# Half chunks at the start, two norms let past VectorE's splits, and a softmax mask moved from TensorE to VectorE

## The reference, cut to what matters

```python
for i in range(2):
    sh0, sc0, g0, sh1, sc1, g1, sh2, sc2, g2 = split(silu(c) @ mod_w[i] + mod_b[i], 9)
    x = x + 0.5 * g0 * swiglu(modulate(rms_norm(x, norm_g[i, 0]), sh0, sc0), ...)
    x = x + g1 * mixer(modulate(rms_norm(x, norm_g[i, 1]), sh1, sc1))   # pool, then attention
    x = x + 0.5 * g2 * swiglu(modulate(rms_norm(x, norm_g[i, 2]), sh2, sc2), ...)
x = rms_norm(x, final_g)
...
# the last layer's mixer: a causal attention of 8 heads of 64, beside an mLSTM branch
s_own = einsum('bhqd,bhkd->bhqk', qi, k_own) * scale
p = softmax(where(causal, s_own, -inf))
```

## Time and profile before

| what | value |
|---|---|
| median of 3 runs | 1464.5 us (1461.75 to 1464.64) |
| the profiled execution's own time | 1464.01 us |
| its span, first to last instruction | 1462.4 us |
| TensorE products busy | 1378.3 us, 94% of the span |
| VectorE busy | 931.0 us, 64% |
| ScalarE busy | 630.4 us, 43% |
| GpSimd busy | 179.5 us, 12% |
| TensorE waited for GpSimd's 1/rms matrix (L641 behind L2675) | 20.6 us in 6 waits |
| TensorE waited for the first chunk of `mod_w` (L612) | 10.0 us |
| TensorE waited for a chunk's sum on VectorE (L603 behind L1865) | 9.6 us in 2 waits |
| TensorE waited for the low part of an activation (L493 behind L2099) | 6.2 us in 3 waits |

### The profile page before, as it was taken

How to read it: one execution, slowest core, us unless ns; L and a number is a source line. 1 busy time by engine, 2 the same in 40 slices (tenths; PEclk the granted TensorE clock), 3 DMA queues, 4 the chain that set the end, 5 groups by cost and what they waited for, 6 DMA issues and landing times.

```text
span 1462.4 us, 18060 instructions
## 1 busy us (share of the span) xinstructions
PE 1378.3 (94%) x6431; PEld 1119.9 (77%) x6431; DVE 931.0 (64%) x1084; ACT 630.4 (43%) x821; POOL 179.5 (12%) x233
## 2 busy tenths in 40 slices
PE   6979999799999999999999799999799999999997
PEld 3668887688887788887777578888687777888885
DVE  4677777767777667777666465564677546555542
ACT  2433334443333544333565453433554645544341
POOL 2010002210001200011133010001208000000000
PEclk9989999899999999999999899999999999999999
DMA  9898886197886588884543275555436434455540
GB/s 337 283 333 293 297 304 226 58 326 278 298 297 216 180 309 288 288 303 139 165 140 95 85 281 173 184 193 189 145 116 209 144 124 136 157 175 177 198 170 29
DMA packets 179910, 304.82 MB, mean 208 GB/s; under 512 B 8516, under 2 KB 122580, under 8 KB 179592
## 3 DMA queue, kind: packets, MB, share of 16 engines
q1 hardware_dynamic: 159272, 224.62, 45.3%
q0 software_dynamic: 20576, 79.37, 15.0%
HBM read 302.91 MB, written 1.05 MB: 208 GB/s over the span
## 4 chain that ended last, share of the span: by engine, by line
PE 44%; DVE 3%; ACT 2%; POOL 1%; issue 1%; DMA 1%; SPq 0%; POOLq 0%; DVEq 0%; ACTq 0%
PE ps L493 13%; PE ps L495 12%; PE ps L494 12%; PE ps L641 1%; DVE wlo L1824 1%; PE ps L904 1%; PE ps L924 1%; PE ps L585 0%; ACT whi L1258 0%; PE ps L1147 0%; DMA raw<-in_ffn_w_gu 0%; DVE xres L2064 0%; DVE xn L2061 0%; DMA raw<-in_w_gate_up 0%; PE ps L1035 0%
## 5 line engine op out<-in xcount | busy, mean ns | idle before, releaser
L1824 DVE TENSOR_TENSOR wlo<-raw,whi 128x2048 fp32r<-128x2048 f32 x212 | 483.0, 2309 | 82.6 <-ACT whi L1258 82.4
L493 PE MATMUL ps<-whi,nthi 128*128 128x512 f32 (+1 forms) x1264 | 509.2, 403 | 7.8 <-DVE ntlo L2099 6.2
L494 PE MATMUL ps<-wlo,nthi 128*128 128x512 f32 (+1 forms) x1264 | 497.1, 393 | 0.0
L495 PE MATMUL ps<-whi,ntlo 128*128 128x512 f32 (+1 forms) x1264 | 496.4, 393 | 0.0
L1258 ACT ACTIVATE whi<-raw 128x2048 fp32r<-128x2048 f32 x212 | 397.0, 1909 | 83.8 <-DMA raw<-in_ffn_w_gu 41.9
L493 PEld LDWEIGHTS ps<-whi,nthi 128*128 128x128 f32 x1264 | 241.4, 191 | 58.4 <-issue 7.3
L495 PEld LDWEIGHTS ps<-whi,ntlo 128*128 128x128 f32 x1264 | 241.1, 191 | 51.7
L494 PEld LDWEIGHTS ps<-wlo,nthi 128*128 128x128 f32 x1264 | 241.7, 191 | 46.6 <-issue 0.2
L1865 DVE SCALAR_TENSOR_TENSOR arena<-arena,cact 128x512 f32<-128x512 f32 x238 | 181.9, 764 | 9.4
L493 PE MATMUL ps<-whi,hthi 128*128 128x512 f32 x440 | 174.8, 397 | 3.4 <-DVE htlo L1906 3.4
L495 PE MATMUL ps<-whi,htlo 128*128 128x512 f32 x440 | 172.1, 391 | 0.0
(11 more groups left out here) (252 smaller groups left out, 919.5 us busy)
## 6 DMA issues: line engine op xcount, KB each, us to landing
raw<-in_ffn_w_gu SPq DMA_DIRECT2D x176, 512.0 KB, 4.8
arena<-in_mod_w POOLq DMA_DIRECT2D x72, 1024.0 KB, 7.8
raw<-in_ffn_w_down SPq DMA_DIRECT2D x88, 512.0 KB, 5.8
raw<-in_w_in SPq DMA_DIRECT2D x44, 512.0 KB, 4.4
raw<-in_w_gate_up SPq DMA_DIRECT2D x44, 512.0 KB, 4.7
raw<-in_diff_w_qkv SPq DMA_DIRECT2D x24, 512.0 KB, 4.7
raw<-in_w_down SPq DMA_DIRECT2D x22, 512.0 KB, 5.6
raw<-in_diff_w_o SPq DMA_DIRECT2D x8, 512.0 KB, 4.1
```

The source lines that it names most:

```text
L493: pe.matmul(o, hi, wh, start=start, stop=False)
L494: pe.matmul(o, hi, wl, start=False, stop=False)
L495: return pe.matmul(o, lo, wh, start=False, stop=stop)
L1824: v.tensor_tensor(wlo[:, s * PIECE:(s + 1) * PIECE], raw[:, r * PIECE:(r + 1) * PIECE], hi, ALU.subtract).then_inc(w_lo, 1)
```

## The change

Four edits, and the moves of splits that go with them.

1. **Halves of chunks.** GpSimd's queue loads the first halves of chunks 2 and 0, then the second halves (before: chunk 0, then chunk 2); `load_gu` of piece 0 waits for the third of these four transfers, as before. Chunk 4 is added up in two halves in the middle of `first_head`, chunk 5 in two halves with a split between them at the end of `first_head`, and chunk 6 in two halves around `inner()` of the first step. Piece 3's split moves ahead of `keep_own_chunk`, the others move accordingly; there are 11 splits as before.
2. **The pool join.** The split at the end of `pool()` on VectorE goes to the end of `pool_join`, and between `joined(1)` and the first split VectorE waits for 1/rms of the first half.
3. **The join before the last mixer.** After `joined(1)` VectorE does `normalized(1)` at once and waits for the second 1/rms of that half; of the two splits ahead of it one comes after it and one later, after `keep(1, 0)`.
4. **The mask.** `scores(h)` loses the two mask products. `masked(h)` adds the mask in PSUM to both diagonal blocks in one operation of 128x256 values and waits for it before the maxima.

```diff
@@ scalar, first_head
                 n.next(M)
+                split(1)
                 act.wait_ge(xt_done, 4)
                 scaled_tiles(4, 2)
                 half_hi(0, 1)
                 half_hi(1, 1)
-                split(2)
+                split(1)
                 gated_half(0, full(T))
+                split(1)
                 gated_half(1, full(M))
...
@@ vector, first_head
                 add_chunk(3)
-                split(1)
+                split(2)
                 keep_own_chunk(chunk_at(*MOD_FIRST[1]))
                 keep_chunk(chunk_at(*MOD_FIRST[3]))
...
-                split(2)
+                split(1)
                 pass_by(T)
                 product(0, T)
+                c = add_chunk(halves=(0,))
                 pass_by(M)
                 product(1, M)
                 hidden_lo(0, 0, T)
+                split(1)
                 n.next(A)
                 product(0, A)
-                split(1)
                 hidden_lo(1, 0, M)
+                add_chunk(halves=(1,), of=c)
                 n.next(B)
                 product(1, B)
                 hidden_lo(0, 1, A)
                 split(1)
                 hidden_lo(1, 1, T)
                 split(1)
-                add_chunk()
-                split(1)
                 keep_chunk(chunk_at(*MOD_HEAD[0]))
+                c = add_chunk(halves=(0,))
+                split(1)
+                add_chunk(halves=(1,), of=c)
                 split(2)

             def ffn_steps(f):
-                if MOD_STEP[f]:
-                    add_chunk()
                 if len(MOD_STEP[f]) == 2:
                     keep_chunk(chunk_at(*MOD_STEP[f][0]))
-                    add_chunk()
-                inner()
+                    c = add_chunk(halves=(0,))
+                    inner()
+                    add_chunk(halves=(1,), of=c)
+                else:
+                    if MOD_STEP[f]:
+                        add_chunk()
+                    inner()
                 inner_lo(0)
...
@@ vector, pool_join
                 joined(0, last, (M, M))
-                n.next("rstd")
                 joined(1, last, (M, M))
+                dve.wait_ge(rstd_done, n.next("rstd").at + 1)
                 n.next("rstd")
                 split(1)
                 first_half(0, j, scol[:, :], shift)
                 x_lo(0)
-                split(2)
+                split(3)
...
@@ vector, join
                 joined(1, last, gated)
+                if final:
+                    normalized(1)
+                    dve.wait_ge(rstd_done, n.seen("rstd") + 1)
                 split(splits[2])
-                if final:
-                    normalized(1)
...
@@ vector, second_mix and masked
                 keep(1, 0, full(B))
-                split(2)
+                split(3)
...
                     o = full(A)
+                    diag = o.rearrange("p (a b k) -> p a b k", a=2, b=2)[:, :, 0, :]
+                    own.link(v.tensor_tensor(diag, diag, mask_q.unsqueeze(1).to_broadcast([P, 2, P]), ALU.add))
+                    own.wait()
                     own.link(v.tensor_reduce(top[:, c:c + 1], o[:, 0:P], AX.X, ALU.max, negate=True))
...
@@ tensor, scores
-                    pe.matmul(o[:, 0:P], qTa[rows, 0:P], kTa[rows, 0:P], start=True, stop=False)
-                    pe.matmul(o[:, 0:P], ident[:, :], mask_q, start=False, stop=True)
-                    pe.matmul(o[:, P:3 * P], qTa[rows, P:S], kTa[rows, 0:S], start=True, stop=False)
-                    pe.matmul(o[:, 2 * P:3 * P], ident[:, :], mask_q, start=False, stop=True).then_inc(filled[A], 1)
+                    pe.matmul(o[:, 0:P], qTa[rows, 0:P], kTa[rows, 0:P], start=True, stop=True)
+                    pe.matmul(o[:, P:3 * P], qTa[rows, P:S], kTa[rows, 0:S], start=True, stop=True).then_inc(filled[A], 1)
...
@@ gpsimd, the first transfers
-            for j in (0, 2):
-                load_own_chunk(*MOD_FIRST[j], j)
+            for h in range(2):
+                for j in (2, 0):
+                    load_own_chunk(*MOD_FIRST[j], j, halves=(h,))
```

More of the change, by code:

```diff
@@ L415, in ffn @@
                 if f == 0:
-                    load_gu(gu, 0, 0, [(first_landed[2][0], 16)])
+                    load_gu(gu, 0, 0, [(first_landed[2][1], 16)])
                     load_gu(gu, 1, 0)
@@ L1382, in ffn_head @@
                 one_hi(1, 0)
-                split(1)
+                split(2 if f == 1 else 1)
                 gated_half(0, full_at(A, p + 1))
@@ L1434, in first_head, with blocks_head @@
                 hidden_hi(0, 1, A)
-                split(2)
+                split(1)
                 hidden_hi(1, 1, T)
-                split(3)
-            def blocks_head(j, g_cols, p, keep):
+                split(4)
+            def blocks_head(j, g_cols, p, keep, ahead=1):
                 keep(0, 0, full(A))
@@ L1444, in blocks_head @@
                 pass_by(B)
-                split(1)
+                split(ahead)
                 keep(0, 1, full_at(A, p + 1))
@@ L1662, in others @@
                     nc.scalar.activation(dst, ps[:, 2 + (b + 1) % 2, :], func).then_inc(blk_read[1], 1)
-                blocks_head(j, (g_cols, None), START["in"], keep)
+                blocks_head(j, (g_cols, None), START["in"], keep, 2)
                 n.next(M)
@@ L1790, in _ @@
             norm = scol, mod_cols(0, 6)
-            j = join(*norm, (1, 0, 0, 2))
+            j = join(*norm, (0, 0, 0, 2))
             at = ffn(1, j, norm, True)
@@ L1802, in _ @@
             norm = cols[:, C_MIX:C_MIX + KT], None
-            j = join(*norm, (2, 1, 1, 1), squared=2, tail=at)
+            j = join(*norm, (2, 1, 1, 0), squared=2, tail=at)
             second_mix(j, norm[0])
@@ L1981, in first_head @@
                 split(1)
[L1982 removed]
+                keep_chunk(chunk_at(*MOD_HEAD[0]))
+                c = add_chunk(halves=(0,))
                 split(1)
[L1984 removed]
+                add_chunk(halves=(1,), of=c)
                 split(2)
             def ffn_steps(f):
[L1988 to L1989 removed]
                 if len(MOD_STEP[f]) == 2:
                     keep_chunk(chunk_at(*MOD_STEP[f][0]))
[L1992 to L1993 removed]
+                    c = add_chunk(halves=(0,))
[5 more added lines that the diff above has]
+                    inner()
                 inner_lo(0)
@@ L2141, in join @@
                 joined(1, last, gated)
-                split(splits[2])
                 if final:
                     normalized(1)
+                    dve.wait_ge(rstd_done, n.seen("rstd") + 1)
+                split(splits[2])
                 n.next("rstd")
@@ L2597, in _ @@
             ffn(3, j, norm, True)
-            j, norm = join(cols[:, C_MIX:C_MIX + KT], None, splits=(1, 1, 2), last=START["in"] - 1, final=True, tail=True)
+            j, norm = join(cols[:, C_MIX:C_MIX + KT], None, splits=(1, 1, 1), last=START["in"] - 1, final=True, tail=True)
             second_mix(j, norm)
@@ L2626, in load_chunk, with load_own_chunk @@
                         .then_inc(mod_landed[mod_place(c.first)][h], 16)
-            def load_own_chunk(layer, chunk, i, behind=()):
+            def load_own_chunk(layer, chunk, i, behind=(), halves=(0, 1)):
                 src = d["mod_w"][layer].rearrange("(k p) n -> p k n", p=P)
-                for h in range(2):
+                for h in halves:
                     if behind:
```

1 line of the change is left out of this document (removed).

## The result

| | before | changed |
|---|---|---|
| median | 1464.57 us (1461.75 to 1465.31, 4 runs) | 1454.33 us (1452.05 to 1454.67, 4 runs) |
| span of the profiled execution | 1462.4 us | 1452.6 us |
| products of 512 columns that took 0.60 to 0.66 us (half clock) | 72 | 56 |

The ratio is 0.9930, with an interval of 0.9916 to 0.9944. The kernel is 10.2 us faster. The forecast was 1448.8 us, a gain of 15.2, in a range of 1442 to 1458. The direction and the range held; the gain was forecast half as large again as it is.

The account below looks back on a forecast made before the run. TensorE, busy for 94% of the span, was taken as the bound, so only removing its work or waits pays. Terms: -5.0 - 3.4 - 0.9 - 5.9 = -15.2 us; 1464.0 - 15.2 = 1448.8 us, range 1442 to 1458.

Parts of the forecast that it names:

- The start, forecast -5.0: Halves of chunks at the start: later first product, no wait for chunk 4, earlier chunk 6; -5.0 us, bounds 0 and -9.
- the sum of chunk 6: At the start, TensorE's sum of chunk 6 comes at 97.3 instead of 103.72, with VectorE as the bound: -6.4 us.
- The pool join, forecast -3.4: Pool join: GpSimd's matrix is done at 278.8 instead of 282.3; -3.4 us, bounds -1.2 and -5.0.
- the matrix goes in between the last join operation and the split: Pool join: GpSimd's matrix runs after VectorE's last join operation and before its split, done at 278.2 + 0.6 = 278.8.
- meets the split: Pool join, lower bound: GpSimd's matrix collides with VectorE's split, and the edit gives only -1.2 us.
- piece 38: Behind the pool join: its load goes out later but lands before ScalarE's gated half, so no cost was put for it.
- The last join, forecast -0.9: Join before the last mixer: normalized(1) starts 3.0 us earlier, the matrix loses 2.1 to a split; -0.9 us, bounds -0.9 and -3.0.
- the tie: Last join: VectorE's split and GpSimd's matrix start on the same signal; the split was taken to win, +2.1 us.
- Rival (a): Last join: the matrix wins the tie by issue order, another -2.1 us, 1446.7 us; chance 20%.
- The mask, forecast -5.9: Last mixer: TensorE saves 0.75 us a head in eight heads by losing the mask products; -5.9 us, bounds -4.4 and -6.0.
- The cover: Last mixer: VectorE's 2.03 us wait before each head's split hides the added mask operation; only 0.1 given back at head 1.
- Rival (b): The start gives nothing, since waits for chunks 5 and 6 move to transfers: 1453.8 us; chance 18%.

Follow-up runs that it names:

- mask_only: The kernel before with only the mask edit, the mask added in PSUM by VectorE: 1455.07 us, ratio 0.9950.
- start_only: The kernel before with only the halves of chunks at the start, joins and mask as before: 1461.22 us, ratio 0.9976.
- no_pool_join: The changed kernel with the pool join as before (split ahead of the join operations, no wait for 1/rms): 1456.26 us, ratio 0.9937 to the kernel before.
- matrix_first: The changed kernel, but VectorE waits in both joins until GpSimd's matrix is done, not only 1/rms: 1450.36 us, ratio 0.9907 to the kernel before.
- quarter_lo: The changed kernel with the low part beside the matrix made in four operations instead of one in both joins: 1452.30 us, ratio 0.9916 to the kernel before.

## Why the prediction was right, and where it wasn't

**The start, forecast -5.0.** The steps came as written: first product 2.4 us later (2.9 said), the kept chunk waited for, no wait for chunk 4, the sum of chunk 6 within 0.9 us of its forecast, half clock behind it (from -7.3 at chunk 6 to -4.6 at the loop, a loss of 2.7 where 1.4 was put). But the term is mis-sized. It was priced against one execution of the kernel before, in which a piece landed 3.2 us later than in mask_only and which stands 2.5 us behind that one at 121 us. Over all profiles the edit is worth about 2.0 us at 121 us, and by the times of start_only 3.5 (1.9 to 5.1). Of the changed kernel's own 4.6, 1.7 went again at the end of the first part: the same wait of 1.39 us at 221 left the clock at full (1.00) where in the kernel before it was half (0.54 from 227 to 230), but TensorE only met its next wait sooner, 1.68 us for VectorE's product at 232.67, and the half level came there. Four kernels with the same two waits kept the clock, so this loss can stay away; what decides it is open.

**The pool join, forecast -3.4.** This is the step that failed, "the matrix goes in between the last join operation and the split". The mean fell into the join operation that reads PSUM, as said, and the power began in its last 0.1 us, and that was too early: 1/rms was done before the last operation, so VectorE never stood still, and there was no gap for the matrix. It "meets the split", which was the bound of -1.2; the squares at 288 moved by 1.2. A second step failed unseen: what waits behind the join was priced at nothing. The text looked at piece 38 alone, and no wait of TensorE came of that one. But ScalarE's moved high part (piece 39) held its low part back by 1.38 us and with it the load of piece 42 (310.64), and that load held the gated half: 2.0 to 3.75 us were given back. From 261 to 338 us the changed kernel's two profiles lose 2.5 and 0.8 us. Four profiles with the join as before (no_pool_join, start_only, mask_only and the kernel before) moved by -0.4 to 0.9 in this stretch. By the profiles the edit gave nothing or cost a little; by the times the changed kernel and its repetition are 1.0 to 1.6 us ahead of no_pool_join, inside the noise. Its worth as a whole stays open, and 3.4 us is in neither.

**The last join, forecast -0.9.** Right in its mechanism: the tie was lost, 2.70 us, wait 1.0 shorter. 0.5 was kept; part of the rest went into transposes of 3.79 instead of 3.43 us. Rival (a), the matrix wins, didn't occur, but forced by a wait in matrix_first its 2.1 us were all there, and 0.5 more (0.4 of it in shorter transposes, 3.41 us). By the Trainium skill (SBUF — State Buffer, Who interferes with whom) the shared ports belong for a whole instruction to whoever issues first. Here VectorE was first, by 0.07 us, and the trace agrees; the near tie of the earlier trace rows remains the other way round.

**The mask, forecast -5.9.** 6.7 us, in all kernels with it but quarter_lo (5.5; why is open). The cover was there: the addition took 0.43 us, close to the earlier trace rows, and of TensorE's longer waits only the one behind head 1's exponentials grew, from 0.30 to 0.48 us, about the 0.1 that was put for it. The size is 0.84 us a head instead of 0.75, since I took only the two starts of the mask products: the score product between them fell from 0.62 to 0.53 us as well.

**What wasn't in the sum.** This part is luck. 2.1 us between 338 and 1041 us came without an edit, 1.6 of them at 668 to 678, where the kernel before had a stretch below full clock (0.88 and 0.95) and the changed one none. The forecast had 15.2 us, the profile has 9.8. The excess of 5.4 is the pool join with what lies behind it (5.9: 3.4 forecast, 2.5 lost), the start (2.1: 5.0 and 2.95) and the last join (0.4), less the mask (0.8) and this drift (2.1). Rival (b), that the start gives nothing, named 1453.8 us and is nearest in number, but not by its mechanism: the start did give. That the total came within the range owes something to errors that cancel, the mask and the drift against the start and the pool join.

## What to carry to other kernels

When a small GpSimd operation is the last link before TensorE, let VectorE wait for that last link and not for the one before it: a wait on 1/rms instead of on the matrix left TensorE waiting 2.1 us longer in each join. A split has two halves on two engines, and a load waits for the second. When you move one, follow it on both, up to the load that it frees and to whoever waits for that load: here a high part moved on ScalarE delayed a load, and with it TensorE, some 40 us behind the join. And before a gain is measured against one trace, look at what in that trace may be luck: two executions of the same instructions differed by 2.5 us, as much as this edit was worth.

## What the hardware showed that I hadn't expected

The half level of TensorE's clock doesn't follow from one wait alone. After the same wait of 1.38 and 1.39 us at the same place the clock was 0.54 in the one kernel and 1.00 in the other, and after the next wait of 1.68 us it fell in eight profiles and not in four.

VectorE's work on one piece keeps GpSimd out for its whole length as one operation (2.70 us), but not as four that follow without a gap (1.62 us). Yet in the pool join GpSimd's matrix stayed out through the rest of one operation and the whole of the next, different one (3.28 us, in both profiles of the changed kernel). What tells these cases apart no run here shows.
